# Three transformer blocks on one core: moving the second product of each modulation row behind the turn of the probabilities

## The chip, the cores and the metric

The kernel runs on one core of one Trainium2 chip. A core has engines that run side by side and each take their own instructions in order: TensorE (PE; its weight loads are shown apart as PEld), VectorE (DVE), ScalarE (ACT), GpSimd (POOL) and the queue engine SyncE (SP). They meet only at semaphores. The metric is the time of one execution on the device in microseconds, as a median over runs.

## The reference

One token sequence of 256 rows of 1024 float32 values goes through three blocks.

- Block one: six modulation vectors `mod = silu(c) @ w_ada + b_ada` (6 x 1024), a normed and modulated input, a mixer of sliding-window attention with sinks and of gated linear attention, an output projection, and 32 experts of which each token takes 4.
- Block two: one wide input projection, an attention with three branches (compressed, selected and windowed keys) and a block attention, a depthwise convolution of width 31 with layer norm and silu, a linear attention with decays (HGRN2), an output projection, a feed-forward part of width 4096.
- Block three: retention, latent attention and 32 small experts in four groups. It is modulated as block one is, with its own 6 x 1024 vectors from `w_ada_3`.

What the change touches, cut down:

```python
mod  = jax.nn.silu(c) @ w_ada[l] + b_ada[l]            # blocks one and three
p    = masked_softmax(s, mask);  o = p @ v             # window, compressed, selected, block attention
h    = conv(a * sigmoid(g)) + b_dw                     # block two, 31 taps
h    = silu(layer_norm(h, ln_g, ln_b)) @ w_pw
attn = einsum('bhtk,bhsk,bhtsk->bhts', q, k, decay)    # block two, decay = exp(cum_t - cum_s)
o    = o * rsqrt(mean(o * o)) ;  o * norm_g * sigmoid(g)
```

## The kernel before, in words

The order of every engine is written by hand; there is no scheduler. The four programs (`block.tensor`, `block.scalar`, `block.vector`, `block.sync`) walk through the same stages. Matrix products of general use land in three PSUM banks in rotation. PE's `bank()` waits until the product three back has been read, and `close()` raises `product_ready`; on ACT, `product()` waits for the next one and `read()` copies it out and raises `product_free`. So the products of PE and the reads of ACT must come in one and the same order. Weights come in slabs of 2 MB over SP, into three rotating places, and a slab is fetched when the products of the slab three back are done.

Attention is done in units: 4 in block one (`attention(0, n_window, ...)`) and 8 in block two (kinds cmp, sel, win, moba for the first 128 rows, then again for the second 128). A unit takes four heads:

- PE makes the scores (L892); DVE scales, masks and finds the negative maximum (`shift`, L2069 to L2080); ACT takes exponentials (L1607); PE turns the probabilities with transposes (L908); ACT copies them from PSUM (L1616); PE multiplies by the values (L917); DVE divides by the sums (`finish`, L2100).
- PE makes the scores of unit u+1 before it turns unit u. Between them each engine has a hook, a function of the unit's number (`rest_of_modulation`, `between_units`, `between_windows`), that does other work.

The hook on PE is mostly a modulation row of 512 values: `mod_parts` multiplies the slab of w_ada by the conditioning vector (32 + 4 matmuls, L854 and L859), ACT reads the result in quarters into one small buffer (L1554, 128x128), and then `mod_spread` copies it to all partitions with four matmuls (L867), which ACT reads into MOD (L1554, 128x512). Block one does two rows in each unit, block two one row.

In block two the hooks also carry the linear attention. DVE: `spans` (L2119, L2120) in hook 0, `parts` (L2148, L2150) in hook 1, `weigh_parts` (L2155, L2156) in hook 3, `weigh_spans` (L2126, L2127) in hook 4, `merge` (L2167 to L2179) in hook 7, and eight taps of the convolution (L2426) in each of the hooks 0 to 6, four in hook 7. ACT: all exponentials of the decays in hook 2 (`decays`, L1622 to L1628). PE: `linear_diagonal` (L938) in hook 4, `linear_masked` (L953) in hook 5, `linear_wide` (L962 to L976) in hook 6. Behind the last unit PE turns the convolution (L1297), makes the linear outputs (L987), waits for the norm on DVE (L1984 to L2457) and the silu on ACT (L1841), turns that (L1304), multiplies it by `conv_pw_w`, and turns the joined features Y (L786) for the output projection.

Of the kernel before, what the change touches and what calls it, by code (L numbers as in the profile page):

```python
# [12 lines left out]
P = 128  # L13
# [139 lines left out]
def build(nc, I, out, rel_scratch):  # L153
    first, end, first_slab, release = product_plan()
    landed = landed_plan()
    with ExitStack() as ctx:
# [599 lines left out]
        def _(pe):  # L756
# [85 lines left out]
            def modulation(name, j, i):  # L842


                mod_parts(first_slab[name] + i - (4 if name == "ada1b" else 0), j, i)
                mod_spread(done[0], ada_quarters[j])
# [53 lines left out]
            def attend(u):  # L900
                kind, t, grp, nk, width = units[u]
                pe.wait_ge(att["probs"], u + 1)
                if u >= 1:
                    pe.wait_ge(att["turned_copied"], u)
                for kt in range(-(-nk // P)):
                    n = min(P, nk - P * kt)
                    for h in range(4):
                        mm = pe.transpose(ps[0:n, 6 + kt, P * h:P * (h + 1)], sP[:, h, P * kt:P * kt + n], ident[:, :])  # L908
                mm.then_inc(att["turned"], 1)
                pe.wait_ge(att["turned_copied"], u + 1)  # L910
                if u >= 1:
# [9 lines left out]
            def attention(u0, u1, between=lambda i: None):  # L921

                scores(u0)
                for u in range(u0, u1):
                    if u + 1 < u1:
                        scores(u + 1)
                    between(u - u0)
                    attend(u)
# [138 lines left out]
            def rest_of_modulation(i):  # L1067
                if i == 2:
                    centered_products()
                for x in range(2):  # L1070
                    modulation("ada1b", 0, 4 + 2 * i + x)
# [211 lines left out]
            def between_units(i):  # L1283
                modulation("ada3", 1, i)
                if i == 4:
                    linear_diagonal(1)
                if i == 5:
                    linear_masked(1)
                if i == 6:
                    linear_wide(1)  # L1290

            attention(n_window, n_window + n_nsa, between_units)
            pe.wait_ge(conv_ready, 1)
            b = bank()
            for a in range(NT):
                for c in range(2):
                    mm = pe.transpose(b[:, S * a + P * c:S * a + P * (c + 1)], CACC[:, c, P * a:P * (a + 1)], ident[:, :])  # L1297
            close(mm)
# [236 lines left out]
        def _(act):  # L1535
# [57 lines left out]
            def modulation(j, i):  # L1593
                read(ada_quarters[j], product()[:, 0:P])
                read(MOD.rearrange("p m d -> p (m d)")[:, BANK * i:BANK * (i + 1)], product())
# [23 lines left out]
            def decays(n):  # L1619

                act.wait_ge(lin["spans"], n + 1)
                act.activation(KL, KL, ACT.Exp)  # L1622
                for i in range(len(WIDE), len(LEVELS)):
                    act.activation(span_keys(i), span_keys(i), ACT.Exp)
                act.activation(QL, QL, ACT.Exp)
                act.activation(lin_tiles[n]["QN"], lin_tiles[n]["QN"], ACT.Exp).then_inc(lin["span_exp"], 1)
                act.wait_ge(lin["parts"], 1)
                act.activation(LD, LD, ACT.Exp).then_inc(lin["part_exp"], 1)  # L1628
# [190 lines left out]
            def between_units(i):  # L1819
                modulation(1, i)  # L1820
                if i == 2:
                    decays(1)
# [4 lines left out]
                if i == 6:  # L1827
                    linear_wide()

# [124 lines left out]
        def _(dve):  # L1954
# [32 lines left out]
            def inverse_roots(n, eps, square=False, first=0):  # L1987

# [6 lines left out]
                tell(dve.tensor_scalar(var[:, 0:n], variance, eps, None, ALU.add), var_ready, roots[0])  # L1995
                dve.wait_ge(std_ready, roots[0])
# [436 lines left out]
            def between_units(i):  # L2433
                taps(i)
# [16 lines left out]
            for a in range(NT):  # L2451
                moments(CTOK[:, a, :], a)
            inverse_roots(NT, 1e-5)
# [219 lines left out]
```

## Time and profile before

| | us |
|---|---|
| median of 3 runs | 2463.42 (2462.71 to 2465.99) |
| the profiled execution | 2463.65 |
| its span in the profile | 2461.6 |
| PE busy | 2060.4 (84%) |
| DVE busy | 494.8 (20%) |
| ACT busy | 364.7 (15%) |
| POOL busy | 322.6 (13%) |

The shares are means over stages with different limits. The two stretches that the change touches are 126 to 189 us (four attention units of block one) and 1389 to 1503 us (eight units of block two and what follows up to the output projection). In the timeline a row begins with its start in us and its length; a bracket at its end tells how long the engine stood idle before it and which instruction ended that. A row of 4 matmuls of float32 is shown as 8 passes in some lines. Instructions of PE overlap by some 0.1 us, so the next start says more than the length.

### The profile page before, as it was taken

Reading aid. Unit: us, or ns where it says so; the run is one execution under the profiler, and the core shown is the slowest. Engines: PE = TensorE matmul, PEld = TensorE weight load, DVE = VectorE, ACT = ScalarE, POOL = GpSimd, SP = SyncE. Lnnn points to the kernel's source line nnn. Section 1 sums busy time; section 2 is a strip of 40 time slices with the busy share of each in tenths; the row PEclk is TensorE's granted clock in tenths of the full one; section 3 lists DMA queues with packets and bytes.
Section 4 is the critical chain, followed back from the end, with each engine's and each line's share of the span. In section 5 each row is a group of like instructions: output and inputs, shape, how many; then the busy total and the mean of one; then the engine's idle time right before and its main releaser. Section 6 shows DMA issues by size and latency. Waiting matters only on the chain.

```text
span 2461.6 us, 34558 instructions
## 1 busy us (share of the span) xinstructions
PE 2060.4 (84%) x14185; PEld 1144.0 (46%) x14186; DVE 494.8 (20%) x1075; ACT 364.7 (15%) x808; POOL 322.6 (13%) x149
## 2 busy tenths in 40 slices
PE   6986698668768866989869788999989899889788
PEld 5764222112212211322238665889875546455444
DVE  1034411101111100211120474110221301241111
ACT  1231111011111100111111432100011112210001
POOL 4100112222222222221220000000000000002221
PEclk9988799889989988999989978999989999989889
DMA  9665679999999799997974642655534244259994
GB/s 325 169 240 216 278 302 407 426 426 418 408 426 399 313 425 425 380 407 310 414 302 137 222 155 84 225 166 152 183 118 136 103 141 150 104 203 404 410 409 158
DMA packets 183320, 681.49 MB, mean 277 GB/s; under 512 B 15970, under 2 KB 57219, under 8 KB 150224
## 3 DMA queue, kind: packets, MB, share of 16 engines
q1 hardware_dynamic: 179200, 670.02, 69.8%
q0 software_dynamic: 4032, 10.40, 1.7%
q8 instruction: 58, 0.95, 0.2%
q14 instruction: 14, 0.11, 0.0%
q10 hardware_dynamic: 16, 0.02, 0.0%
HBM read 679.33 MB, written 1.06 MB: 276 GB/s over the span
## 4 chain that ended last, share of the span: by engine, by line
PE 65%; DMA 23%; DVE 6%; ACT 3%; SPq 2%; issue 1%; POOL 0%; DVEq 0%; ACTq 0%; POOLq 0%
PE ps L775 33%; DMA scr<-in_w_mlp 13%; PE ps L1153 8%; PE ps L1179 5%; DMA MOD<-in_w_mlp 3%; DMA spare<-in_b_mlp 3%; PE ps L1470 2%; PE ps L1190 2%; DMA HTY<-in_w 2%; PE ps L810 2%; PE ps L854 1%; PE ps L1121 1%; PE ps L1157 1%; PE ps L917 1%; PE ps L1507 1%
## 5 line engine op out<-in xcount | busy, mean ns | idle before, releaser
L1153 PE MATMUL ps<-ring,scr 128*32 128x512 f32 x2208 | 300.2, 693 | 132.2 <-POOL ring L721 131.8
L775 PE MATMUL ps<-ring,HTY 128*128 128x512 f32 (+5 forms) x960 | 326.3, 501 | 3.7 <-ACT HTY L1554 3.7
L721 POOL COPY ring<-scr 128x4096 f32<-128x4096 f32 x62 | 224.1, 3619 | 776.5 <-DMA scr<-in_w_mlp 569.5
L775 PEld LDWEIGHTS ps<-ring,HTY 128*128 128x128 f32 x960 | 174.7, 190 | 152.0 <-issue 136.0
L775 PE MATMUL ps<-HTY,ring 128*128 128x256 f32 (+1 forms) x1072 | 238.3, 385 | 2.0 <-ACT HTY L1554 1.0
L1153 PEld LDWEIGHTS ps<-ring,scr 128*32 128x32 f32 x2208 | 74.1, 122 | 352.5 <-POOL ring L721 180.4
L775 PEld LDWEIGHTS ps<-HTY,ring 128*128 128x128 f32 (+1 forms) x1072 | 205.5, 192 | 33.3 <-ACT HTY L1554 2.7
L2359 DVE TENSOR_SCALAR spare<-ps 128x256 f32<-128x256 f32 x46 | 19.5, 425 | 675.2 <-PE ps L1157 675.2
L1554 ACT ACTIVATE scr<-ps 128x512 f32<-128x512 f32 (+7 forms) x117 | 58.4, 500 | 503.8 <-PE ps L775 401.6
L775 PE MATMUL ps<-ring,scr 128*128 128x128 f32 (+1 forms) x1040 | 121.6, 280 | 1.4 <-DVE scr L2465 1.4
L775 PEld LDWEIGHTS ps<-ring,scr 128*128 128x128 f32 x1040 | 117.5, 192 | 5.2 <-issue 3.3
L1153 PE MATMUL ps<-MOD,scr 128*32 128x512 f32 x736 | 90.9, 612 | 28.0 <-DMA MOD<-in_w_mlp 19.2
L1747 ACT ACTIVATE spare<-spare 128x256 f32<-128x256 f32 x46 | 19.1, 416 | 590.1 <-DVE spare L2359 590.1
L752 POOL COPY scr<-MOD 128x4096 f32<-128x4096 f32 x7 | 26.0, 3717 | 566.2 <-PE ps L1470 452.6
L1179 PE MATMUL ps<-scr 128*32 128x512 f32 x736 | 88.5, 598 | 7.1 <-DMA scr<-in_w_mlp 7.1
L1470 PE MATMUL ps<-scr,BIAS 128*32 128x512 f32 x432 | 73.2, 675 | 23.8 <-POOL scr L752 23.1
L1190 PE MATMUL ps<-spare,scr 64*128 64x512 f32 x368 | 91.4, 615 | 0.8 <-ACT spare L1757 0.8
L1179 PE MATMUL ps<-HTY,scr 128*32 128x512 f32 x736 | 90.1, 608 | 0.0
L775 PEld LDWEIGHTS ps<-spare,H 128*128 128x128 f32 x320 | 75.4, 329 | 9.2 <-issue 7.5
L775 PE MATMUL ps<-spare,H 128*128 128x128 f32 x320 | 77.3, 402 | 1.6 <-DVE spare L2579 1.6
L854 PE MATMUL ps<-ring,cols 128*32 128x128 f32 x1472 | 56.1, 316 | 18.1 <-DMA ring<-in_w_ada 18.1
L1153 PEld LDWEIGHTS ps<-MOD,scr 128*32 128x32 f32 x736 | 23.7, 112 | 89.3 <-issue 55.3
(461 smaller groups left out, 1940.4 us busy)
## 6 DMA issues: line engine op xcount, KB each, us to landing
scr<-in_w_mlp SPq DMA_DIRECT2D x94, 2048.0 KB, 25.5
ring<-in_w_mlp SPq DMA_DIRECT2D x34, 2048.0 KB, 20.9
MOD<-in_w_mlp SPq DMA_DIRECT2D x32, 2048.0 KB, 24.3
HTY<-in_w_mlp SPq DMA_DIRECT2D x32, 2048.0 KB, 22.2
ring<-in_w_ada SPq DMA_DIRECT2D x23, 2048.0 KB, 9.1
ring<-in_w_in SPq DMA_DIRECT2D x20, 2048.0 KB, 7.9
ring<-in_w_ff SPq DMA_DIRECT2D x16, 2048.0 KB, 9.5
ring<-in_w SPq DMA_DIRECT2D x16, 2048.0 KB, 16.3
```

The source lines that it names most:

```text
L721: pool.tensor_copy(m1_slabs[j], m1_arrivals[j]).then_inc(moved[j], 1)
L752: pool.tensor_copy(m3_slabs[j], m3_arrivals[j]).then_inc(moved[j], 1)
L775: mm = pe.matmul(o, lhs(k), rhs(k), start=begin and k == 0, stop=end and k == nk - 1)
L810: mm = pe.matmul(b[64 * half:64 * half + 64, S * i:S * (i + 1)], c[half](k), rhs[:, k, :], start=k == 0, stop=k == nk - 1)
L854: pe.matmul(b[32 * t:32 * (t + 1), 0:P], csil[:, j, k:k + 1].to_broadcast([P, 32]), w[:, k, P * t:P * (t + 1)], start=k == 0, stop=False)
L917: mm = pe.matmul(ps[:, 3, h * width:(h + 1) * width], sPT[0:n, kt, h, :], values_of(u, kt, h), start=kt == 0, stop=kt == kts[-1])
L1121: mm = pe.matmul(ps[C1 * q:C1 * (q + 1), 3, 0:S], PICK[:, a, :], H[:, a, S * q:S * (q + 1)], start=a == 0, stop=a == NT - 1)
L1153: mm = pe.matmul(ps[C1 * c:C1 * (c + 1), 0, :], XG[:, 2 * j + i, :], m1_slabs[j][:, i, BANK * c:BANK * (c + 1)], start=j + i == 0, stop=False)
L1179: mm = pe.matmul(ps[r:r + C1, 1, :], aT[:, i, C1 * c:C1 * (c + 1)], m1_slabs[j][:, 2 * t + i, BANK * half:BANK * (half + 1)], start=j + i ...
L1190: mm = pe.matmul(sum_bank(a, half), GPT[r, P * a:P * (a + 1)], YS[r, :], start=False, stop=last, skip_group_check=True)
L1470: mm = pe.matmul(ps[32 * t:32 * (t + 1), 0, :].rearrange("p (x f) -> p x f", x=2), XG3[:, 4 * h + i, C3 * t:C3 * (t + 1)], m3_slabs[2 * h ...
L1554: act.activation(dst, src, func, **kw).then_inc(product_free, 1)
```

## The change

Four edits in the hooks.

1. A modulation row's second product (`row_spread`) is taken out of the hook and goes between the turn of the probabilities and their product with the values (`within`). In block one this is so for the second of a unit's two rows; in block two for each unit's row. ACT reads the spread row one hook later (or behind the attention, for the last).
2. Block two, ACT: `decays` is cut in three: the keys' (`key_decays`) in hook 1, the parts' (`part_decays`) in hook 2, the queries' (`query_decays`) in hook 3.
3. Block two, DVE: the last taps go into hook 6 (12 instructions there, none in hook 7), and `merge` from hook 7 to hook 6.
4. Block two: the turn of the convolution and its read go into hook 7 of PE and ACT, in front of the last turn of probabilities. DVE takes the moments in hook 7 and offers the variances there, ACT takes the root in front of the linear outputs' reads.

```diff
@@ PE
-            def modulation(name, j, i):
+            def row_parts(name, j, i):
                 mod_parts(first_slab[name] + i - (4 if name == "ada1b" else 0), j, i)
-                mod_spread(done[0], ada_quarters[j])
+                return done[0]
+            def row_spread(parts, j):
+                mod_spread(parts, ada_quarters[j])
...
-            def attend(u):
+            def attend(u, within):
...
                 mm.then_inc(att["turned"], 1)
+                within()
                 pe.wait_ge(att["turned_copied"], u + 1)
...
-                    between(u - u0)
-                    attend(u)
+                    attend(u, between(u - u0))
...
             def rest_of_modulation(i):
                 if i == 2:
                     centered_products()
-                for x in range(2):
-                    modulation("ada1b", 0, 4 + 2 * i + x)
+                row_spread(row_parts("ada1b", 0, 4 + 2 * i), 0)
+                parts = row_parts("ada1b", 0, 5 + 2 * i)
+                return lambda: row_spread(parts, 0)
...
             def between_units(i):
-                modulation("ada3", 1, i)
+                parts = row_parts("ada3", 1, i)
...
+                if i == 7:
+                    turn_convolution()
+                return lambda: row_spread(parts, 1)
@@ ACT
-            def decays(n):
-                act.wait_ge(lin["spans"], n + 1)
+            def key_decays():
+                act.wait_ge(lin["spans"], 2)
                 act.activation(KL, KL, ACT.Exp)
...
+            def query_decays():
                 act.activation(QL, QL, ACT.Exp)
...
+            def part_decays():
                 act.wait_ge(lin["parts"], 1)
                 act.activation(LD, LD, ACT.Exp).then_inc(lin["part_exp"], 1)
...
             def rest_of_modulation(i):
+                if i >= 1:
+                    row_spread(3 + 2 * i)
...
-                modulation(0, 4 + 2 * i)
-                modulation(0, 5 + 2 * i)
+                row_parts(0)
+                row_spread(4 + 2 * i)
+                row_parts(0)
             attention(0, n_window, rest_of_modulation)
+            row_spread(11)
...
             def between_units(i):
-                modulation(1, i)
+                if i >= 1:
+                    row_spread(i - 1)
+                row_parts(1)
+                if i == 1:
+                    key_decays()
                 if i == 2:
-                    decays(1)
+                    part_decays()
+                if i == 3:
+                    query_decays()
...
+                if i == 7:
+                    read(CTOK[:, :, :], two(product()))
...
             attention(n_window, n_window + n_nsa, between_units)
-            read(CTOK[:, :, :], two(product()))
+            row_spread(7)
+            root(2)
             linear_outputs(Y[:, :, 768:], 64)
-            root(2)
@@ DVE
-                for k in range(1 + each * i, min(CONVW, 1 + each * (i + 1))):
+                for k in range(1 + each * i, 1 + each * (i + 1) if i < 6 else CONVW):
...
-                taps(i)
+                if i < 7:
+                    taps(i)
...
+                if i == 6:
+                    merge(1, end["in_tile3"] - 1)
                 if i == 7:
-                    merge(1, end["in_tile3"])
+                    dve.wait_ge(product_free, end["ada3b"] - 4)
+                    for a in range(NT):
+                        moments(CTOK[:, a, :], a)
+                    offer_variances(NT, 1e-5)
             attention(n_window, n_window + n_nsa, between_units)
-            dve.wait_ge(product_free, end["ada3b"] - 3)
-            for a in range(NT):
-                moments(CTOK[:, a, :], a)
-            inverse_roots(NT, 1e-5)
+            take_roots(NT)
```

On PE, in a unit of block one with 256 keys, the order was (parts of the second row, its spread, turn, values):

```order
L854 MATMUL ps<-ring,cols 32x128 x32
L859 MATMUL ps<-scr,ident 32x128 x4
L867 MATMUL ps<-scr,ident 128x128 x4
L908 MATMUL ps<-ident,scr 128x128 x8
L917 MATMUL ps<-scr 128x64 x8
```

and is now, with the spread (L869) behind the turn (L910):

```order
L856 MATMUL ps<-ring,cols 32x128 x32
L861 MATMUL ps<-scr,ident 32x128 x4
L910 MATMUL ps<-ident,scr 128x128 x8
L869 MATMUL ps<-scr,ident 128x128 x4
L920 MATMUL ps<-scr 128x64 x8
```

So PE's wait for the read of the quarters falls behind the turn, and the spread stands where PE waited for ACT's copy.

On PE in block two, unit 4 of the attention (compressed keys, second half of the rows) before, with `linear_diagonal` at L938:

```order
L854 MATMUL ps<-ring,cols 32x128 x32
L859 MATMUL ps<-scr,ident 32x128 x4
L867 MATMUL ps<-scr,ident 128x128 x4
L938 MATMUL ps<-heads,HTY 128x2 x16
L908 MATMUL ps<-ident,scr 15x128 x4
L917 MATMUL ps<-scr 128x64 x4
```

and now:

```order
L856 MATMUL ps<-ring,cols 32x128 x32
L861 MATMUL ps<-scr,ident 32x128 x4
L940 MATMUL ps<-heads,HTY 128x2 x16
L910 MATMUL ps<-ident,scr 15x128 x4
L869 MATMUL ps<-scr,ident 128x128 x4
L920 MATMUL ps<-scr 128x64 x4
```

The spread stood in front of the diagonal products, which wait for DVE; it now stands behind them.

On ACT in block two, from the copy of unit 7's probabilities to the silu of the convolution, before (read of the turned convolution, two reads of linear outputs, table and root, table and silu):

```order
L1616 ACTIVATE scr<-ps 128x1024
L1554 ACTIVATE scr<-ps 128x512
L1554 ACTIVATE HTY<-ps 128x256 x2
L1563 ACT_TABLE_LOAD
L1563 ACTIVATE stat<-stat 128x2
L1841 ACT_TABLE_LOAD
L1841 ACTIVATE scr<-scr 128x512
```

and now, from the read of the turned convolution:

```order
L1563 ACTIVATE scr<-ps 128x512
L1627 ACTIVATE scr<-ps 128x1024
L1563 ACTIVATE MOD<-ps 128x512
L1572 ACT_TABLE_LOAD
L1572 ACTIVATE stat<-stat 128x2
L1563 ACTIVATE HTY<-ps 128x256 x2
L1869 ACT_TABLE_LOAD
L1869 ACTIVATE scr<-scr 128x512
```

The root and its table moved in front of the reads of the linear outputs, and the read of the convolution in front of the last copy.

## Rows read from the trace of the kernel before

**Rows 1.** The page: its span, and the chain that ended last, by engine.
```profile
span 2461.6 us, 34558 instructions
...
PE 65%; DMA 23%; DVE 6%; ACT 3%; SPq 2%; issue 1%; POOL 0%; DVEq 0%; ACTq 0%; POOLq 0%
```

**Rows 2.** Timeline of PE, block one: start, length, instruction, [idle before <-releaser].
```profile
133.02 1.16 PE L867 MATMUL ps<-scr,ident 128*128 128x128 f32 x8 [0.40 <-ACT scr L1554]
134.02 0.60 PE L908 MATMUL ps<-ident,scr 128*128 128x128 f32 x4
135.35 1.10 PE L917 MATMUL ps<-scr 128*128 128x64 f32 x8 [0.74 <-ACT scr L1616]
...
167.60 1.04 PE L908 MATMUL ps<-ident,scr 128*128 128x128 f32 x8
169.75 2.04 PE L917 MATMUL ps<-scr 128*128 128x64 f32 x16 [1.11 <-ACT scr L1616]
```

**Rows 3.** Waits of PE from 1386 to 1506 us: total, times, longest.
```profile
PE ps L917 <- ACT scr L1616: 12.0, 8, 5.8
```

**Rows 4.** Timeline of DVE, block two.
```profile
1392.03 0.88 DVE L2069 SCALAR_TENSOR_TENSOR scr<-ps,BIAS 128x256 f32<-128x256 f32 x2 [1.66 <-PE ps L892]
...
1403.09 0.42 DVE L2120 TENSOR_TENSOR scr<-scr 128x256 f32<-128x256 f32 x1
...
1413.15 1.23 DVE L2150 TENSOR_SCALAR HTY<-HTY 128x2048 f32<-128x2048 f32 x1
...
1433.06 1.23 DVE L2156 TENSOR_TENSOR HTY<-HTY,scr 128x1024 f32<-128x1024 f32 x1
...
1447.32 0.42 DVE L2127 TENSOR_TENSOR scr<-scr 128x256 f32<-128x256 f32 x1
...
1478.32 0.42 DVE L2100 TENSOR_TENSOR scr<-ps,stat 128x256 f32<-128x256 f32 x1 [9.58 <-PE ps L917]
...
1481.32 0.69 DVE L2167 TENSOR_TENSOR scr<-scr,diag 128x512 f32<-128x512 f32 x1
...
1487.91 0.17 DVE L2090 TENSOR_SCALAR stat<-stat 128x4 f32<-128x4 f32 x1
```

**Rows 5.** Timeline of ACT, block two, unit 2.
```profile
1414.41 1.91 ACT L1628 ACTIVATE HTY<-HTY 128x2048 f32<-128x2048 f32 x1
```

**Rows 6.** Timeline of PE, block two, units 2 to 7 and behind them.
```profile
1416.86 1.97 PE L917 MATMUL ps<-scr 128*128 128x64 f32 x8 [5.81 <-ACT scr L1616]
...
1434.34 3.75 PE L938 MATMUL ps<-heads,HTY 128*128 128x2 f32 x32
...
1439.64 1.97 PE L917 MATMUL ps<-scr 15*128 15x64 f32 x8 [0.68 <-ACT scr L1616]
...
1448.82 3.39 PE L953 MATMUL ps<-scr,H 64*128 64x64 f32 x32
...
1454.34 3.12 PE L917 MATMUL ps<-scr 128*128 128x64 f32 x16 [1.11 <-ACT scr L1616]
...
1474.54 3.67 PE L917 MATMUL ps<-scr 128*128 128x64 f32 x16 [1.11 <-ACT scr L1616]
...
1488.19 1.23 PE L987 MATMUL ps<-scr,H 128*128 128x64 f32 x10
...
1502.52 3.67 PE L786 MATMUL ps<-ident,HTY 128*128 128x128 f32 x16 [0.69 <-ACT HTY L1554]
```

**Rows 7.** Timeline of ACT behind the last unit of block two.
```profile
1491.42 1.28 ACT L1563 ACT_TABLE_LOAD   x1
1492.71 0.20 ACT L1563 ACTIVATE stat<-stat 128x2 f32<-128x2 f32 x1
...
1495.56 0.63 ACT L1841 ACTIVATE scr<-scr 128x512 f32<-128x512 f32 x1 [1.35 <-DVE scr L2457]
```

**Rows 8.** Timeline of SP: the first fetch of expert weights.
```profile
195.81 0.37 SPq L496 DMA_DIRECT2D scr<-in_w_mlp  x1
```

**Rows 9.** Busy time by stretch: length, PE, PEld, DVE, ACT, POOL, granted clock, DMA share, GB/s.
```profile
260.00:1200.00 940.00, 740.96 (x5774) 222.74 (x5770) 143.38 (x376) 109.57 (x258) 209.65 (x58) 0.91 0.92 386
1386.00:1489.00 103.00, 85.95 (x1022) 66.84 (x1019) 78.56 (x170) 37.45 (x112) 0.00 (x0) 0.78 0.54 190
```

More of the change, by code:

```diff
@@ L919, in attend, with attention @@
                 mm.then_inc(att["out"], 1)
-            def attention(u0, u1, between=lambda i: None):
+            def attention(u0, u1, between=lambda i: lambda: None):
                 scores(u0)
@@ L1290, in between_units, with turn_convolution @@
                     linear_wide(1)
-            attention(n_window, n_window + n_nsa, between_units)
-            pe.wait_ge(conv_ready, 1)
-            b = bank()
-            for a in range(NT):
-                for c in range(2):
-                    mm = pe.transpose(b[:, S * a + P * c:S * a + P * (c + 1)], CACC[:, c, P * a:P * (a + 1)], ident[:, :])
-            close(mm)
+                if i == 7:
+                    turn_convolution()
+                return lambda: row_spread(parts, 1)
+            def turn_convolution():
+                pe.wait_ge(conv_ready, 1)
+                b = bank()
+                for a in range(NT):
+                    for c in range(2):
+                        mm = pe.transpose(b[:, S * a + P * c:S * a + P * (c + 1)], CACC[:, c, P * a:P * (a + 1)], ident[:, :])
+                close(mm)
+            attention(n_window, n_window + n_nsa, between_units)
             linear_outputs(1, IH, 64)
@@ L1591, in diagonal, with row_parts, row_spread @@
                 read(BD[64:P, first_slot:first_slot + n, 1, :], v[64:P])
-            def modulation(j, i):
+            def row_parts(j):
                 read(ada_quarters[j], product()[:, 0:P])
+            def row_spread(i):
                 read(MOD.rearrange("p m d -> p (m d)")[:, BANK * i:BANK * (i + 1)], product())
@@ L1624, in decays @@
                     act.activation(span_keys(i), span_keys(i), ACT.Exp)
+            def query_decays():
                 act.activation(QL, QL, ACT.Exp)
-                act.activation(lin_tiles[n]["QN"], lin_tiles[n]["QN"], ACT.Exp).then_inc(lin["span_exp"], 1)
+                act.activation(lin_tiles[1]["QN"], lin_tiles[1]["QN"], ACT.Exp).then_inc(lin["span_exp"], 1)
+            def part_decays():
                 act.wait_ge(lin["parts"], 1)
@@ L1987, in inverse_roots, with offer_variances @@
             def inverse_roots(n, eps, square=False, first=0):
+                offer_variances(n, eps, square, first)
+                take_roots(n, first)
+            def offer_variances(n, eps, square=False, first=0):
                 mean, variance = (moment[:, 2 * first + i:2 * (first + n):2] for i in range(2))
@@ L1995, in inverse_roots, with take_roots @@
                 tell(dve.tensor_scalar(var[:, 0:n], variance, eps, None, ALU.add), var_ready, roots[0])
+            def take_roots(n, first=0):
                 dve.wait_ge(std_ready, roots[0])
@@ L2445, in between_units @@
                     weigh_spans(1, QH, FH)
+                if i == 6:
+                    merge(1, end["in_tile3"] - 1)
                 if i == 7:
-                    merge(1, end["in_tile3"])
+                    dve.wait_ge(product_free, end["ada3b"] - 4)
+                    for a in range(NT):
+                        moments(CTOK[:, a, :], a)
+                    offer_variances(NT, 1e-5)
             attention(n_window, n_window + n_nsa, between_units)
-            dve.wait_ge(product_free, end["ada3b"] - 3)
-            for a in range(NT):
-                moments(CTOK[:, a, :], a)
-            inverse_roots(NT, 1e-5)
+            take_roots(NT)
             for a in range(NT):
```

## The prediction

> **What bounds the kernel now.** I read the page first: the chain that ended last is 65% PE and 23% DMA, with little DVE [rows 1]. Then the timelines of the stretches that the change touches. In block one PE never stands for longer than a read of ACT: it waits 0.40 us for the quarters in front of each spread, and 0.74 us (128 keys) or 1.11 us (256 keys) for the copy of the turned probabilities in front of L917 [rows 2]. PE is the bound there, and each of these waits is on the path. In block two the same wait adds up to 12.0 us in 8 units, but one of the eight is 5.8 us long [rows 3], so a mean over units misleads. DVE's timeline tells why: from 1392.03 us to the end of the parts at 1414.38 (1413.15 + 1.23) it has no gap, and ACT starts the exponential of the parts at 1414.41, 0.03 us later; behind its 1.91 us comes the copy that releases PE at 1416.86 [rows 4 to 6]. The first units of block two are bound by DVE. DVE delivers twice more: the weighed parts at 1434.29 (1433.06 + 1.23), the weighed spans at 1447.74. PE takes the first at 1434.34 and the second only at 1448.82 [rows 4, 6]. Later DVE stands idle for 9.58 us [rows 4]: units 6 and 7 are bound by PE. What follows, from the linear outputs at 1488.19 to the turn of Y at 1502.52, is a chain of 14.33 us through DVE and ACT [rows 6, 7].
>
> **Block one.** Nothing is added; two things change place. Unit with 128 keys, before: from the end of the second row's parts, 0.40 us of wait, 1.00 us of spread (133.02 to 134.02), 1.33 us of turn and copy (134.02 to 135.35) [rows 2], in all 2.73. After: the turn first, four transposes at half of what eight take (1.04 us, less an overlap of 0.16: 0.44), in which ACT reads the quarters, then 1.00 us of spread, 1.44 in all, just beyond the 1.33 of turn and copy. Gain 1.29 us. Unit with 256 keys: before 0.40 + 1.00 + 2.15 (167.60 to 169.75) = 3.55 us; after, turn 0.88 plus spread 1.00 is 1.88 and hides in the 2.15. Gain 1.40. Two of each: 5.4 us. ACT's deferred read of the spread row stands behind the next unit's exponentials, where it waits for PE anyway; it would cost PE only if it delayed the next read of quarters. The bounds are 0 (ACT or a slab of weights becomes late each time) and 7.0 us (each unit gets the wait of 0.40, the spread of 1.00 and 0.35 more).
>
> **Block two, units 0 to 2.** The gains of the same kind are lost. The parts' end on DVE does not depend on anything that moves, and 1.91 us of exponential and the copy follow as before, so unit 2's L917 stays at 1416.86 [rows 4 to 6]. Cutting the decays in three removes nothing: what is taken out of hook 2 stood in the shade of the wait for the parts. It adds a wait instead: the keys' decays in hook 1 wait for the spans, ready at 1403.51 (1403.09 + 0.42) [rows 4]; queued behind them on ACT is unit 1's copy, so PE gets a new stop of some 5 us in unit 1. It ends near 1405.5 and costs nothing as long as unit 2's turn is there by 1416: some 7 us of PE's work in 11 us.
>
> **Units 3 and 4.** Whatever unit 3 gains (about 1.2 us) is lost at the diagonal products, which cannot start before 1434.29; PE took them at 1434.34 already. Behind them the spread now stands where it was in the shade: before, turn and copy took 1439.64 - 1434.34 - 3.6 = 1.7 us [rows 6]; after, turn 0.9 (at the lower clock) and spread 1.0 to 1.1. I take a loss of 0.3 us.
>
> **Units 5 to 7.** Unit 5: PE reaches the masked products 1.40 us sooner, less that 0.3, but the weighed spans come at 1447.74 against 1448.82: gain 1.0 us, and the rest of the unit as in block one. L917 of unit 5 at about 1453.3. Unit 6: 1.40 us again, less up to 0.6 where the clock is low and the spread outlasts the copy: 1.2. Unit 7: 1.40; the turn of the convolution moves in front of the turn at the same price. Sum 3.6 us at the linear outputs, 1488.2 becomes 1484.6. Two additions on DVE hide: four more taps and the merge in hook 6. The merge takes 6.6 us (1481.32 to 1487.91) and the gap before unit 6's L2100 is 9.58 us [rows 4]. If that cover failed, unit 7's values would wait for unit 6's read; the slack is the some 6 us of unit 7's parts and turn.
>
> **Behind the last unit.** Call the start of the linear outputs L. Before, silu started at 1495.56 = L + 7.4 and ended at L + 8.0 [rows 6, 7]. Now the convolution is read in hook 7, the variances wait for no one, and table and root are done by about L. DVE needs its division of unit 7 and then root, centring and gain: L + 2.9. ACT must read the linear outputs first (until 1491.42 - 1488.19 = L + 3.2), load the silu table, 1.28, and run 0.63 us [rows 7]: L + 5.1. So 2.9 us, and the 6.3 us from there to the turn of Y stay. The head norm is ready about a microsecond before it is asked for.
>
> The sum: 5.4 + 3.6 + 2.9 = 11.9 us. The profiled execution took 2463.65 us, 2.0 more than its span and 0.2 above the median of 2463.42. It becomes 2451.7, a median of 2451.5. Nothing between may swallow it: the expert loop's first fetch is issued at 195.81, released by DVE behind the attention [rows 8], so the stream of weights begins sooner by the same amount, as do all later slabs, which PE's products release.
>
> ACT's table loads are weighed once more. The row shows 1.28 us, and the root starts 1.29 us after the load does [rows 7]. The Trainium skill (ScalarE: Activation LUTs, "What ACT_TABLE_LOAD costs") says that a switch of sets costs the load and a drain, about 2.66 us together. By that the silu would end at L + 6.5 and the sum would be 10.5.
>
> **The rivals.**
> (a) Forecast, 2451.5: chance 0.62.
> (b) Block one's gain does not arrive, because the expert loop is held by the stream: DMA is 92% busy at 386 GB/s for 940 us [rows 9]. Against it: what releases the stream moves too. Then 2463.4 - 6.5 = 2456.9. Chance 0.10.
> (c) DVE holds block two to its end (12 taps and the merge in one hook, or the stop in unit 1 outlasts its cover), and only block one and the tail pay: 5.4 + 2.9 = 8.3, 2455.1. For it: DVE is busy 78.6 of 103 us [rows 9]. Against it: the gap of 9.58. Chance 0.11.
> (d) The clock helps. It was granted at 0.78 in these 103 us [rows 9], so some 44% of the time at 1.2 GHz, 38 us of PE's work. Fewer and shorter stops in units 5 to 7 and in the tail might put a third of it at 2.4: 6 us more, 2445.5. Chance 0.09.
> (e) Slower, by one mechanism: the clock falls. There are now two stops of about 5 us in a row (units 1 and 2) and one of 2 to 3 us in front of the diagonal products. If PE then stays at 1.2 GHz, each microsecond of work that ran at 2.4 takes one more. At 2.4 GHz were 56% of the 86 us, 48 us; those behind unit 2, seven tenths, are not covered by DVE: 34 us. From 11.9 us on the kernel is slower; at half of them, 17 us, it takes 2468.6. After the one stop of 5.81 us before, the clock came back: L917 took 1.97 us for 8 passes there and 1.10 in unit 0 of block one [rows 2, 6], but the mean of the stretch is 0.78. Chance 0.04. The Trainium skill (TensorE: Matmul & The Clock Gate, "HAM oscillation — how this bites in real kernels") warns of just this: waits between bursts of matmuls throttle the engine, and the next burst begins at the low clock each time. The trace agrees as far as one long stop goes; whether two do it is open.
> (f) The page's drain is real on this path, though the row has none: silu 1.4 us later, 2452.9. Chance 0.04.
>
> **How the numbers follow.** The likeliest case gives 2451.5, with 2449 to 2454 of its own for the clock. For eight in ten I take in (b), (c) and (f) and most of (d): 2446 to 2457.5; (e) and the ends are left out. A measurement here tells 0.2% (4.9 us) from no change, so faster means below 2458.5. (a), (c), (d) and (f) are faster, (b) nearly always: 0.90; the same 0.06, from (b) and the edge of (e); slower 0.04.
>
> **What would show it.** In block one, L920 with no idle time in front, and the linear outputs 5.4 us sooner. In block two, a new wait of unit 1 for ACT of 4 to 5 us, unit 2's L920 at the same distance from the first scores, the diagonal products waiting 2 to 3 us for DVE, the masked ones none, merge inside the gap, and the wait for silu 2.5 us instead of 5.3. The prediction is wrong if the granted clock between the units' start and the linear outputs falls well under 0.78, if a DMA wait appears in front of L856, or if the first expert fetch does not move.

## The result and the profile after

| | before | changed kernel |
|---|---|---|
| median | 2463.42 us | 2443.97 us (5 runs, 2436.99 to 2448.2) |
| ratio to before | | 0.9913 (95% interval 0.9897 to 0.9930) |
| span of the profiled execution | 2461.6 us | 2446.3 us |

The change saves 19.5 us; measured a second time it saved 24.4 us (2439.76 against 2464.2, ratio 0.9900, 0.9886 to 0.9915). The forecast was 11.9 us, 2451.5 with 2446.0 to 2457.5. The direction was right; the size lies below the range. It is near the time of rival (d), 2445.5, which had 0.09.

First the parts that came as forecast. PE in block one, a unit of 128 and one of 256 keys (timeline: start, length, instruction, idle time before and its releaser):

```profile
133.15 0.66 PE L910 MATMUL ps<-ident,scr 128*128 128x128 f32 x4
133.65 1.13 PE L869 MATMUL ps<-scr,ident 128*128 128x128 f32 x8
134.61 1.00 PE L920 MATMUL ps<-scr 128*128 128x64 f32 x8
...
166.07 2.00 PE L920 MATMUL ps<-scr 128*128 128x64 f32 x16 [0.22 <-ACT scr L1627]
```

Where L917 waited 0.74 or 1.11 us [rows 2], L920 waits 0 or 0.22. SP issues the first expert fetch at 190.43 us, where it was 195.81 [rows 8]:

```profile
190.43 0.37 SPq L496 DMA_DIRECT2D scr<-in_w_mlp  x1
```

That these are just the 5.4 us of the forecast is luck. The profile of the changed kernel was already 1.71 us later in front of the first edit (first gate product at 114.10, before at 112.39). Counted from there the fetch comes 7.1 us sooner.

PE's waits from 1384 to 1491 us (total, times, longest), which answer to [rows 3]:

```profile
PE ps L920 <- ACT scr L1627: 7.4, 4, 4.8
PE ps L940 <- DVE HTY L2190: 5.4, 1, 5.4
PE ps L1313 <- ACT scr L1869: 2.4, 1, 2.4
PE ps L920 <- DVE scr L2134: 1.7, 1, 1.7
```

The 12.0 us in front of the values have become 9.1, and 5.4 are new in front of the diagonal products. All of PE's idle time from the first scores to the linear outputs, the waits of 0.40 us for the quarters included, is 15.0 us where it was 15.7. Yet this stretch went from 99.4 to 92.96 us: most of the gain is not in the waits. PE's timeline there, to be set beside [rows 6]:

```profile
1385.13 0.63 PE L894 MATMUL ps<-KC,scr 128*128 128x30 f32 x4 [0.39 <-ACT scr L1563]
...
1401.88 1.97 PE L920 MATMUL ps<-scr 128*128 128x64 f32 x8 [4.76 <-ACT scr L1627]
...
1412.99 1.10 PE L920 MATMUL ps<-scr 128*128 128x64 f32 x8 [2.16 <-ACT scr L1627]
...
1430.48 6.98 PE L940 MATMUL ps<-heads,HTY 128*128 128x2 f32 x32 [5.39 <-DVE HTY L2190]
...
1448.01 3.39 PE L955 MATMUL ps<-scr,H 64*128 64x64 f32 x32
...
1453.53 2.00 PE L920 MATMUL ps<-scr 128*128 128x64 f32 x16 [0.22 <-ACT scr L1627]
...
1469.19 2.25 PE L920 MATMUL ps<-scr 128*128 128x64 f32 x16
...
1476.25 2.00 PE L920 MATMUL ps<-scr 128*128 128x64 f32 x16 [0.22 <-ACT scr L1627]
1478.09 1.28 PE L989 MATMUL ps<-scr,H 128*128 128x64 f32 x10
```

Cut the stretch at the values of unit 5. From the first scores to there it takes 68.4 us (1453.53 - 1385.13), where it took 65.55: nothing is gained, 2.85 are lost, chiefly because the 16 diagonal products ran 6.98 us and not 3.75. From there to the linear outputs it takes 24.56 us, where it took 33.85: 9.3 us, and the forecast had 2.6 (units 6 and 7). The view of busy time by stretch shows of what these are made. First the kernel before, then the changed one (length, then busy time of PE, PEld, DVE, ACT and POOL with instruction counts, granted clock, DMA share, GB/s):

```profile
1454.34:1488.19 33.85, 30.83 (x357) 23.82 (x357) 19.20 (x43) 9.64 (x28) 0.00 (x0) 0.70 0.31 109
```

```profile
1453.53:1478.09 24.56, 24.34 (x357) 20.05 (x357) 18.71 (x42) 11.87 (x32) 0.00 (x0) 0.86 0.49 174
```

The same 357 matmuls are busy for 24.34 us in place of 30.83, and the granted clock is 0.86 in place of 0.70. PE stood idle 3.0 us there before and 0.2 us after. So 2.8 us are waits that are gone, which is what the forecast counted, and 6.5 us are the clock. Rows of equal work show where: first the kernel before (scores in unit 5, parts in unit 7), then the changed one.

```profile
1457.26 3.73 PE L892 MATMUL ps<-spare,scr 128*128 128x512 f32 x4
...
1478.15 3.64 PE L854 MATMUL ps<-ring,cols 128*32 128x128 f32 x64
```

```profile
1455.37 1.94 PE L894 MATMUL ps<-spare,scr 128*128 128x512 f32 x4
...
1471.37 1.95 PE L856 MATMUL ps<-ring,cols 128*32 128x128 f32 x64
```

Last the chain behind the units, on ACT, against [rows 7]:

```profile
1476.70 1.28 ACT L1572 ACT_TABLE_LOAD   x1
1478.00 0.20 ACT L1572 ACTIVATE stat<-stat 128x2 f32<-128x2 f32 x1
...
1481.37 1.28 ACT L1869 ACT_TABLE_LOAD   x1
1482.66 0.63 ACT L1869 ACTIVATE scr<-scr 128x512 f32<-128x512 f32 x1
```

From the linear outputs at 1478.09 the silu ends 5.2 us later (forecast 5.1, before 8.0), and PE's turn of it waits 2.42 us in place of 5.3.

### The profile page after: what moved, and what is told of

Its sections match the earlier page's. It is cut to its first block, busy times and chain, and to the rows that moved or that the text cites. A ratio compares the mean times of both kernels' runs of the same rounds, so it can differ in the third digit from the quotient of the medians.

```text
span 2446.3 us, 34558 instructions
## 1 busy us (share of the span) xinstructions
PE 2042.8 (84%) x14185; PEld 1136.4 (46%) x14186; DVE 492.8 (20%) x1075; ACT 363.5 (15%) x808; POOL 321.5 (13%) x149
## 4 chain that ended last, share of the span: by engine, by line
PE 64%; DMA 23%; DVE 7%; ACT 3%; SPq 2%; issue 1%; POOL 0%; DVEq 0%; ACTq 0%; POOLq 0%
PE ps L775 33%; PE ps L1156 9%; DMA spare<-in_b_mlp 8%; DMA scr<-in_w_mlp 7%; PE ps L1182 5%; DMA MOD<-in_w_mlp 4%; PE ps L1479 2%; PE ps L1193 2%; DMA HTY<-in_w 2%; PE ps L810 2%; PE ps L1160 1%; PE ps L1124 1%; PE ps L856 1%; PE ps L1516 1%; PE ps L1490 1%
## 5 line engine op out<-in xcount | busy, mean ns | idle before, releaser
L1156 PE MATMUL ps<-ring,scr 128*32 128x512 f32 x2208 | 294.4, 682 | 134.7 <-POOL ring L721 134.3
L2393 DVE TENSOR_SCALAR spare<-ps 128x256 f32<-128x256 f32 x46 | 19.5, 425 | 680.8 <-PE ps L1160 680.7
L856 PE MATMUL ps<-ring,cols 128*32 128x128 f32 x1472 | 49.1, 290 | 20.0 <-DMA ring<-in_w_ada 20.0
```

The source lines that it names most:

```text
L856: pe.matmul(b[32 * t:32 * (t + 1), 0:P], csil[:, j, k:k + 1].to_broadcast([P, 32]), w[:, k, P * t:P * (t + 1)], start=k == 0, stop=False)
L1156: mm = pe.matmul(ps[C1 * c:C1 * (c + 1), 0, :], XG[:, 2 * j + i, :], m1_slabs[j][:, i, BANK * c:BANK * (c + 1)], start=j + i == 0, stop=False)
```

## The experiments

Three theories from the start. A: the edits pay where they stand; in block two mainly because PE's small waits go and with them the low clock. B: the time comes from another phase of the expert loop's transfers. C: the forecast's sizes hold. Two more later. D: VectorE's work, shortened by the earlier merge, was what held the units. E: the decays' split is what lets the clock rise. Each kernel was profiled; a table behind the experiments puts the stretches side by side.

**Block one's edit alone.** The changed kernel with block two's edits undone.

```diff
-                parts = row_parts("ada3", 1, i)
+                row_spread(row_parts("ada3", 1, i), 1)
...
-                return lambda: row_spread(parts, 1)
+                return lambda: None
```

> Block one's edit alone (the second row's spread behind the turn), block two as before. Theory A (the gain is made where the edits are, and larger than forecast because PE keeps its higher clock longer in these stretches: block one's stretch from the gate's products to the first expert pass took 145.8 us before and 138.6 after, 7.2 less): ratio 0.9971, about -7 us. Theory B (the rest of the gain comes from the expert loop, which runs differently when it starts a few us sooner): 5.4 us from the stretch and some 7 us from the loop, -12 us, 0.995. Theory C (my forecast's size): -5.4 us, 0.9978.

Measured 2458.52 against 2464.2, ratio 0.9977 (0.9965 to 0.9988): 5.7 us, by the interval 3.0 to 8.6. B's 12 us lies outside; the forecast's 5.4 and A's 7 both lie inside, so this run does not part them.

**Block two's edits alone.**

```diff
-                parts = row_parts("ada1b", 0, 5 + 2 * i)
-                return lambda: row_spread(parts, 0)
+                row_spread(row_parts("ada1b", 0, 5 + 2 * i), 0)
+                return lambda: None
```

> Block two's edits alone, block one as before. Theory A: the stretch from the first scores of block two to the turn of Y took 113.7 us before and 104.3 after, so -9.4 us, ratio 0.9962. Theory B: the expert loop of block one starts when it did before, so nothing comes from there; -6.5 to -9 us. Theory C: -6.5 us, 0.9974. Granted clock in the units near 0.83, not 0.78, by A.

Measured 2446.54, ratio 0.9929 (0.9915 to 0.9943): 17.7 us (by the interval 14.0 to 20.9), where the forecast had 6.5 and A had 9.4. All three expectations are too small, and the forecast's error is in block two.

**A delay ahead of the expert loop.** The kernel before, with one squaring on DVE done nine times, between block one's attention and the first expert fetch.

```diff
-                step(dve.tensor_tensor(squares, o, o, ALU.mult))
+                for _ in range(9 if n == 0 else 1):
+                    step(dve.tensor_tensor(squares, o, o, ALU.mult))
```

> The kernel before, with the first DVE instruction of block one's head norm (1.26 us with its step) done nine times in place of once: a delay of 10.1 us ahead of the expert loop, on the chain that sets its start. By A a shift ahead of the loop reaches the end one to one: +10.1 us, 2473.5, ratio 1.0041, all of it standing between the linear outputs and the first expert pass. By B the loop answers to its start: +3 or less, or +17 and more.

Measured 2476.22, ratio 1.0047 (1.0034 to 1.0060). PE's wait there grew by 10.1 us (16.62 for 6.55), the kernel by 12.0 (by the interval 8.4 to 14.8). A shift ahead of the loop goes through it, one to one within that. This is against rival (b), and against B as the source of the whole surprise; it cannot exclude a few us.

**The changed kernel once more**, no edit.

> The changed kernel once more, on this chip, to be compared with the partial ones. All theories: 0.9913 as measured, within 0.003. If it comes out near 0.995 the first measurement was high by chance.

Measured 2439.76, ratio 0.9900 (0.9886 to 0.9915): the first measurement was not high by chance.

**Block two's spread behind the turn, alone.**

```diff
             def between_units(i):
-                modulation("ada3", 1, i)
+                parts = row_parts("ada3", 1, i)
...
+                return lambda: row_spread(parts, 1)
```

> Block two's spread behind the turn, and nothing else (decays in one hook, merge and convolution norm where they were, block one as before). Theory A (the waits that went made the clock of units 5 to 7 rise: in three profiles with all edits the 34 us up to the linear outputs had a granted clock of 0.87 to 0.95, in three without 0.69 to 0.75): the clock there is 0.85 or more, the 34-us stretch's work is done some 8 us sooner, the tail stays at 8.06 us to the turn of the silu; -8 to -11 us in all, ratio 0.996. Theory D (the bound is DVE, and what shortens units 5 to 7 is the merge a unit sooner): -2.6 us or less, clock 0.75 or less.

Measured 2453.44, ratio 0.9956 (0.9939 to 0.9972): 12 us. In its profile the stretch of the units is 89.68 us, as short as with all of the change. Only the tail is longer: PE's turn of the silu comes 11.42 us behind the linear outputs, where the changed kernel has 5.25, since `merge` is still in hook 7 and now late: it ends 3.0 us behind the start of the linear outputs, where it ended 0.3 us ahead of it before the change.

**The decays' split alone.** The recorded expectation names this kernel as the spread with the split. What ran is the split on the order before, without the spread; the numbers expected are not those of this kernel, and it is read here as the split alone.

```diff
+                if i == 1:
+                    key_decays()
                 if i == 2:
-                    decays(1)
+                    part_decays()
+                if i == 3:
+                    query_decays()
```

> As the run with block two's spread alone, and the decays in three hooks as well. Both theories and my forecast: the split of the decays moves a stop from unit 2 to unit 1 and gives nothing, 0 +/- 1 us against the spread alone. A third theory (E: the shorter second stop keeps the clock up and that is where the surprise comes from): 3 us or more better than the spread alone.

Measured 2464.94 against 2465.39, ratio 0.9998 (0.9986 to 1.0010): nothing, as the forecast said of this edit.

**Merge and convolution norm a unit sooner, alone.**

```diff
-                if i == 7:
+                if i == 6:
                     merge(1, end["in_tile3"])
+                if i == 7:
+                    dve.wait_ge(product_free, end["ada3b"] - 3)
...
+                    offer_variances(NT, 1e-5)
```

> Block two's merge and convolution norm a unit sooner, and nothing else (spread in front of the turn, decays in one hook, block one as before). A: the tail is shorter by 2.8 us (5.26 us to the turn of the silu), units 5 to 7 as before: -2.8 us, 0.9989. D: the units get shorter too, -8 us or more in all, 0.9966.

Measured 2463.43, ratio 0.9988 (0.9976 to 1.0001): 2.0 us by the medians, and by the interval anything from nothing to 5.9. The stretch of the units stays long, 104.76 us, so D falls: the earlier merge is not what shortens it. A's tail of 5.26 us did not come either; it is 7.29. PE's wait for the silu fell to 2.42 us as expected, but the linear outputs in front of it took 2.1 us longer, at the lower clock. The two edits need each other: the merge alone is worth about 2 us, behind the spread 6.2 (the tail of 11.42 against 5.26).

**The waits filled, nothing moved.** The kernel before, with 8 idle matmuls between turn and values in units 5 to 7.

```diff
+                if n_window + 5 <= u < n_window + n_nsa:
+                    for _ in range(8):
+                        pe.matmul(ps[:, 3, 256:384], ident[:, :], window[:, 0:P], start=True, stop=True)
                 pe.wait_ge(att["turned_copied"], u + 1)
```

> The kernel before with eight idle matmuls of 128 columns (0.9 us at the higher clock; their result is read by no one) between the turn of the probabilities and PE's wait for their copy, in units 5, 6 and 7 of block two. No work is moved or taken out. A: these three waits of 1.11 us were what held the clock down there; the clock of the 34-us stretch rises above 0.8 and the kernel is 3 to 6 us faster although it does more. D: nothing or +1 us, the clock stays between 0.69 and 0.75.

Measured 2460.56, ratio 0.9976 (0.9961 to 0.9992): faster, though each unit does more. The rows of units 6 and 7 (L914 is the filling), and the busy time of the stretch from unit 5's values to the linear outputs:

```profile
1477.10 1.97 PE L908 MATMUL ps<-ident,scr 128*128 128x128 f32 x8
1478.86 3.01 PE L914 MATMUL ps<-window,ident 128*128 128x128 f32 x16
1481.70 1.90 PE L920 MATMUL ps<-scr 128*128 128x64 f32 x16
...
1488.10 1.95 PE L914 MATMUL ps<-window,ident 128*128 128x128 f32 x16
```

```profile
1461.98:1491.95 29.97, 29.18 (x389) 24.02 (x388) 15.74 (x33) 8.80 (x25) 0.00 (x0) 0.83 0.32 103
```

A filling was expected to take 0.9 us at the higher clock; it took 1.79 and more, since each of its matmuls is two passes. The two fillings of this stretch take 4.6 us (2.84 and 1.79, start to start) in place of 2.2 us of wait. At the old clock the stretch would be 33.85 + 2.4 = 36.3 us; it takes 30.0. So 6.3 us are the clock, 0.83 for 0.70, and no order was changed. That agrees with the 6.5 us above and is the test that carries A. PE's waits of 0.40 us for the quarters were left in this kernel, so it is the waits of 1.11 us that the test bears on. The values of unit 6 (L920, 1.90 us) run at the high level; in [rows 6] the same 16 passes behind the wait of 1.11 us took 3.67.

**Diagonal products a unit later.** The changed kernel with `linear_diagonal` in hook 5, on PE and ACT.

```diff
-                if i == 4:
-                    linear_diagonal(1)
                 if i == 5:
+                    linear_diagonal(1)
```

> The changed kernel with the 16 diagonal products of the linear part (L940) issued in unit 5, ahead of the masked ones, in place of unit 4, on PE and ACT. In the changed kernel PE stops there for 5.4 us (L940, wait for DVE) and then runs the 16 products at the lower clock in 6.98 us, where the kernel before took 3.75. Theory A (PE's short waits and its granted clock set block two): the stop falls to under 1.5 us, block two's stretch from first scores to linear outputs is 2 to 5 us under the changed kernel's 92.8 (88 to 91 us), time 2437 to 2442 us beside the changed kernel's 2440 to 2444. Theory D (VectorE's work sets the stretch): the stop only turns up again at the masked products or at the linear outputs, and the stretch stays at 92 to 94 us. If the 5-us stop had helped the later clock in any way, slower: 94 us and more.

Measured 2445.51, ratio 0.9941 (0.9924 to 0.9959): no better than the changed kernel. A had 88 to 91 us for the stretch from first scores to linear outputs; it is 92.42, as D had it (92 to 94). The stop at L940 is gone and stands at unit 4's values, half as long, since DVE is behind in its own order:

```profile
1429.55 1.07 PE L920 MATMUL ps<-scr 15*128 15x64 f32 x8 [2.69 <-DVE HTY L2132]
...
1436.69 5.24 PE L940 MATMUL ps<-heads,HTY 128*128 128x2 f32 x32
1442.05 6.29 PE L955 MATMUL ps<-scr,H 64*128 64x64 f32 x32
```

**That, and the taps spread otherwise.**

```diff
-                for k in range(1 + each * i, 1 + each * (i + 1) if i < 6 else CONVW):
+                done_taps = (0, 2, 4, 8, 12, 16, 23, 30)
+                for k in range(1 + done_taps[i], 1 + done_taps[i + 1]):
```

> The kernel with the diagonal products in unit 5, and VectorE's convolution taps spread over the hooks as 2, 2, 4, 4, 4, 7, 7 in place of five in each of the first six, so that the linear part's parts, weighed parts and spans come some 4.2 us sooner. Theory A: another 0 to 3 us off the stretch from first scores to linear outputs (86 to 90 us), 2435 to 2441 us in all. Theory D: VectorE's total of work is the same, so its end and the linear outputs stay, and the time is that of the kernel with the products in unit 5 alone, within 1.5 us; the last taps may then turn up as a wait in front of the convolution norm, and cost up to 3 us.

Measured 2442.79, ratio 0.9928 (0.9912 to 0.9944). The units' stretch is the shortest of all, 87.82 us (A had 86 to 90), and DVE is busy for 79.08 of it. So up to unit 5 it is also VectorE's order that sets the pace, as D says; only the merge was the wrong work to name. The whole kernel isn't measurably better than the changed one (A had 2435 to 2441), and in its profile block one happened to take 69.44 us, the longest of the new orders.

**The decays in one hook again, the rest as changed.**

```diff
-                if i == 1:
-                    key_decays()
                 if i == 2:
+                    key_decays()
+                    query_decays()
                     part_decays()
-                if i == 3:
-                    query_decays()
```

> The changed kernel with block two's decays in one hook again, as before the change. Alone, on the order before, the split moved nothing (2464.9 beside 2465.4). Theory A: nothing here too, within 2 us of the changed kernel (2440 to 2446), the stop in units 1 and 2 merely changes its place. Theory E (the shorter second stop through the split is what lets the granted clock rise later): the stretch from first scores to linear outputs goes from 92.8 to 96 us or more, and the time to 2446 to 2450.

Measured 2443.25, ratio 0.9925 (0.9913 to 0.9937): as fast as with the split. E falls; that edit is worth nothing in either order.

**The stop in front of the diagonal products filled.** The changed kernel with 28 idle matmuls (L936).

```diff
+                for _ in range(28):
+                    pe.matmul(ps[:, 7, 0:P], ident[:, :], window[:, 0:P], start=True, stop=True)
```

> The changed kernel with 28 idle 128x128 matmuls into an unused bank, whose result nobody reads, between unit 4's work and the wait for VectorE's weighed parts in front of the diagonal products (L940). Theory A (a stop lowers the granted clock of what follows): with the stop filled, the 16 diagonal products take about 3.7 us in place of 6.98, and the stretch from first scores to linear outputs is 2 to 4 us under 92.8. If the granted clock doesn't depend on PE's own activity before the products: the products stay at 7.0 us, and the stretch stays at 92.8 or grows by what the filling takes beyond the stop (0 to 2 us).

Measured 2445.74, ratio 0.9928 (0.9913 to 0.9944): nothing gained. In the profile the products run at the other level, as A had it, but begin later; the stretch to the linear outputs is 91.85 us, not 2 to 4 us under 92.8:

```profile
1423.63 6.52 PE L936 MATMUL ps<-window,ident 128*128 128x128 f32 x56
1429.99 3.63 PE L942 MATMUL ps<-heads,HTY 128*128 128x2 f32 x32
```

The granted clock of the products, here and in the changed kernel:

```profile
1429.99:1433.48 3.49, 3.49 (x34) 3.49 (x33) 3.26 (x7) 0.00 (x0) 0.00 (x0) 1.00 0.00 0
```

```profile
1430.48:1437.32 6.84, 6.84 (x32) 6.84 (x33) 6.42 (x13) 0.00 (x0) 0.00 (x0) 0.50 0.00 0
```

The same products: 1.00 behind idle matmuls, 0.50 behind 5.39 us of standing. But they begin 48.5 us behind the first scores and not 45.4. DVE ends the weighed parts at 1427.09, 45.6 us behind the first scores, so the filling outlasts the stop by 2.9 us. What the clock gives (3.4 us), the filling takes. A shorter filling wasn't tried. Nor is the length of the stop all that decides: in the filled kernel above, the order before in this place, these products took 6.90 us behind a stop of only 1.04, and with block one's edit alone 4.09 behind 1.16.

**The stretches side by side**, each from one profile, in us. I: block one, from its first gate product (L1034, now L1036) to its linear outputs. II: block two, first scores to unit 5's values. III: from there to the linear outputs. IV: from there to the turn of the silu.

| kernel | I | II | III | IV |
|---|---|---|---|---|
| before | 72.38 | 65.55 | 33.85 | 8.06 |
| block one alone | 66.23 | 67.28 | 32.19 | 8.06 |
| delay | 71.28 | 70.70 | 34.02 | 8.06 |
| split alone | 71.32 | 68.95 | 33.82 | 8.06 |
| merge alone | 71.08 | 70.73 | 34.03 | 7.29 |
| filling (units 5 to 7) | 71.49 | 70.97 | 30.08 | 8.52 |
| changed | 66.91 | 68.40 | 24.56 | 5.25 |
| changed, again | 64.96 | 69.36 | 23.46 | 5.26 |
| block two alone | 71.37 | 66.18 | 23.49 | 5.26 |
| spread alone | 71.19 | 66.18 | 23.50 | 11.42 |
| old decays | 65.01 | 66.15 | 23.48 | 5.26 |

Column III parts the kernels: 32 to 34 us wherever the spread stands in the hook, 23.5 to 24.6 wherever it stands behind the turn, with the filling between. The granted clock parts them in the same way, 0.69 to 0.73 against 0.86 to 0.93. PE is busy 30.6 us there in the mean of the five old orders without filling and 23.3 in the five new ones, with the same matmuls.

## Why the prediction was wrong

The direction held, and so did most steps; one term was mis-sized.

- Block one, 5.4 us: right. Column I is 71.4 us in the mean of seven old orders and 66.5 in seven new ones (65.0 to 69.4, with the three kernels that the table leaves out), 4.9 us; the median said 5.7. Behind it are 1.6 us that the forecast didn't have: linear outputs to the turn take 9.43 us in every new order, and without the delay 11.07 in all but one of the old, again the clock. Not all of it is kept: in four of the kernels with 9.43 or 9.44, among them block one alone, PE takes 2 us longer from that turn to the first expert product (64.3 to 65.1 us in place of 62.3 to 62.6). In the mean 0.7 us remain. Block two alone has 9.44 with block one's old order, so the edit isn't the only thing that brings it. In the profile before the linear outputs ran at 0.62, after at 1.00, with the wait of 6.55 us for DVE behind them the same:

```profile
184.77:189.29 4.52, 4.52 (x26) 4.33 (x25) 0.42 (x1) 0.60 (x1) 0.00 (x0) 0.62 0.02 6
```

```profile
181.01:183.90 2.89, 2.89 (x26) 2.71 (x25) 0.42 (x1) 0.60 (x1) 0.00 (x0) 1.00 0.09 28
```

- Units 0 to 2, nothing: right. The stop of unit 1 is there with 4.76 us, released by ACT, which waited 3.77 us for the spans. Unit 2's values come 27.9 us behind the first scores; before it was 28.1.
- Units 3 and 4: the mechanism was right, the gain was lost in front of the diagonal products. DVE delivers when it did, 45.3 us behind the first scores (before 45.5). The stop is 5.4 us (3.4 with block two alone), not 2 to 3: from unit 2's values on PE needed 12.1 us to reach it and not 17.5, since the parts of unit 3 took 1.95 us in place of 3.64, at the higher clock. And the products behind the stop ran at the lower clock, which cost 3.2 us that the step did not have.
- **The step that failed:** "Unit 6: 1.40 us again, less up to 0.6 where the clock is low and the spread outlasts the copy: 1.2. Unit 7: 1.40 ... Sum 3.6 us at the linear outputs". It priced the waits that go and left all other work at the speed of [rows 6]. Its 1.0 us up to unit 5 is not contradicted by column II, 68.6 in the mean of five old orders and 67.3 of five new ones, but single kernels spread over 5 us there. Column III refutes the 2.6 us of units 6 and 7: 33.6 against 23.7, 9.9 us. About 2.7 of these are the waits, just what the forecast counted, and 7.2 are PE's busy time, which the higher clock shortens. The rows that should have warned were there: the values of unit 6 took 3.67 us [rows 6], those of the same shape 2.04 in block one [rows 2].
- Rival (d) named this, "Fewer and shorter stops in units 5 to 7", and its size of 6 us was near; the fault was its chance of 0.09, and reading the warning of rival (e) for long stops only. The Trainium skill (TensorE: Matmul & The Clock Gate, "HAM oscillation — how this bites in real kernels") says that waits between bursts throttle the engine. The traces agree, and here for waits of only 1.11 us, once in a unit: 0.70 with them, 0.83 with them filled, 0.86 and more with them gone. The prediction took the rule as speaking against this change, and it spoke for it.
- Behind the last unit, 2.9 us: right, 2.8. The table's load took 1.28 us and the function began 1.29 us after it, both times; the load itself began 0.03 us behind the last read (1481.37, the read ended at 1481.34). So the drain that the Trainium skill states (ScalarE: Activation LUTs, "What ACT_TABLE_LOAD costs") is not seen here either; rival (f) falls.
- Rival (b) falls with block one alone and with the delay, (c) with the shorter stretch of units 5 to 7, (e) with column III. The stops of 4.8, 2.2 and 5.4 us did lower the clock behind them, 0.50 at the diagonal products, but it was back before unit 5's values.

By the measured stretches: 4.9 + 0.7 + 1.4 + 9.9 + 2.8 = 19.7 us; the two measurements were 19.5 and 24.4.

Four things stay open. What keeps the clock up in III was shown by filling and by moving the waits, not by putting waits back into the new order; that wasn't tried. Nor were the waits of 1.11 and of 0.40 us taken out one kind at a time. The filling's profile is of its longest execution (2469.8; 12 runs from 2452.2): 6.3 us of clock less 2.4 of added work in units 6 and 7 and 1.05 in unit 5 would be 2.8, and the median gained 4.8 (by the interval 2.0 to 9.6), but whether the clock stays up in each of its executions was not seen. Column II spreads over 5 us, for which no edit accounts. And from the first expert product to the first scores of block two, where all kernels have the same code, PE took 1128.4 us in the mean of eight kernels with the spread of block two moved and 1131.2 in six without: 2.9 us that no theory here explains, and in which B may still have a part.

## What to carry to other kernels

A wait of one microsecond that comes back in every unit can cost several times its length if PE's granted clock around it is low: look at the granted clock and at the same shape's duration in other stretches, and price the work behind the wait at both levels. Moving work that nobody waits for into such a wait was worth more here than filling it, and filling it is a cheap test of what the clock is worth. Edits that look separate should be tried apart and together: here the earlier merge was worth 2 us alone and 6 behind the spread, and the split decays nothing.

## What had not been expected of the hardware

- The clock falls without a wait too. In the changed kernel unit 6's turn behind the many small products of `linear_wide` took 1.97 us and its values 2.25, against 1.09 and 2.00 in unit 5, with no idle time in front:

```profile
1451.33 1.09 PE L910 MATMUL ps<-ident,scr 128*128 128x128 f32 x8
...
1462.84 1.80 PE L972 MATMUL ps<-spare,H 64*64 64x64 f32 x56
1464.57 1.23 PE L978 MATMUL ps<-spare,H 64*128 64x128 f32 x8
1465.72 1.97 PE L910 MATMUL ps<-ident,scr 128*128 128x128 f32 x8
```

  The kernel before has this fall too, in the same place (the second row of 56 passes took 1.89 us, the turn 1.97). What differs is how long it lasts: with the wait of 1.11 us behind the turn the next parts still took 3.64 us, without it 1.95.

- One code has more than one course. From the first scores to the linear outputs the kernel before took 99.40 us, the one with block one's edit alone 99.47, the one with the delay 104.72, with the same instructions there. A difference of 5 us in this stretch between two profiles shows nothing by itself.
- From the first expert product to the first scores of block two the profiles show 1124.98 to 1132.69 us, in kernels that have the same code there. That is 8 us, of the size of what single times of one kernel differ by (2436.99 to 2448.2 for the changed one).
